# Tap sums of the late tokens' first chunks among the gates, layer norm statistics on VectorE, and a reordered convolution tail

## The reference, cut to what matters

```python
def conformer_conv_module(h, w_in, b_in, w_dw, b_dw, ln_g, ln_b, w_out, b_out):
    D = h.shape[-1]
    u = h @ w_in + b_in
    u = u[..., :D] * jax.nn.sigmoid(u[..., D:])
    u = lax.conv_general_dilated(            # 31 taps, each channel by itself, causal
        u, w_dw[:, None, :].astype(u.dtype), window_strides=(1,), padding=[(CONV_WIDTH - 1, 0)],
        dimension_numbers=('NWC', 'WIO', 'NWC'), feature_group_count=D) + b_dw
    u = jax.nn.silu(layer_norm(u, ln_g, ln_b))
    return u @ w_out + b_out
...
x = x + g1[:, None, :] * y                   # y is the module's output
h = modulate(rms_norm(x, norm2_g[layer]), sh2, sc2)
x = x + g2[:, None, :] * moe_ffn(h, ...)
```

## Time and profile before

| | before |
|---|---|
| median of 3 runs | 2340.85 us (2340.23 to 2343.32) |
| the profiled execution | 2344.01 us, span 2342.2 us |
| mean granted TensorE clock | 0.941 |
| busy: PE / DVE / ACT / POOL | 2095.6 / 1156.7 / 676.9 / 348.2 us |
| chain that ended last | PE 82%, DVE 8%, DMA 5%, ACT 2%, issue 2% |
| first gate product of DVE to the last router logits | 1356.5 to 1782.4 us of the span |

### The profile page before, as it was taken

How to read it: one execution, slowest core, us unless ns; L and a number is a source line. 1 busy time by engine, 2 the same in 40 slices (tenths; PEclk the granted TensorE clock), 3 DMA queues, 4 the chain that set the end, 5 groups by cost and what they waited for, 6 DMA issues and landing times.

```text
span 2342.2 us, 51476 instructions
## 1 busy us (share of the span) xinstructions
PE 2095.6 (89%) x19986; PEld 1150.2 (49%) x19987; DVE 1156.7 (49%) x2301; ACT 676.9 (29%) x1654; POOL 348.2 (15%) x609
## 2 busy tenths in 40 slices
PE   6999999999999579999999489997983899999991
PEld 2444444455666345555555367653442455555550
DVE  2355500578898532222322689997735222232225
ACT  3111100567777322222222310006252222222222
POOL 0000010000000122222222330000001222222223
PEclk9999999799999789999999699998986899999996
DMA  9266510103300746658776401232034777734746
GB/s 395 77 244 241 198 55 0 37 19 144 145 10 10 301 147 256 219 203 319 259 287 254 164 0 72 96 101 65 1 126 170 295 292 290 286 120 149 258 149 224
DMA packets 117719, 391.04 MB, mean 167 GB/s; under 512 B 22849, under 2 KB 43969, under 8 KB 112257
## 3 DMA queue, kind: packets, MB, share of 16 engines
q1 hardware_dynamic: 67970, 302.95, 34.1%
q0 software_dynamic: 21632, 67.76, 8.2%
q10 hardware_dynamic: 28032, 19.17, 2.7%
HBM read 337.56 MB, written 47.49 MB: 164 GB/s over the span
## 4 chain that ended last, share of the span: by engine, by line
PE 82%; DVE 8%; DMA 5%; ACT 2%; issue 2%; SPq 1%; POOL 0%; ACTq 0%; DVEq 0%; POOLq 0%
PE ps L1527 21%; PE ps L1541 11%; PE ps L1400 10%; PE ps L1600 7%; PE ps L1671 5%; PE ps L1418 5%; PE ps L1474 4%; PE ps L1432 3%; PE ps L1445 3%; PE ps L1457 3%; DVE kv L1267 3%; PE ps L1519 2%; DMA ring<-in_w_gate_up 2%; PE ps L1534 1%; PE ps L1347 1%
## 5 line engine op out<-in xcount | busy, mean ns | idle before, releaser
L1179 DVE TENSOR_TENSOR hT<-hT,ps 128x128 f32<-128x128 f32 x146 | 42.0, 288 | 546.1 <-ACT hT L732 546.1
L1527 PE MATMUL ps<-ring,hT 128*32 128x256 f32 x4544 | 267.3, 388 | 18.8 <-issue 9.1
L1527 PE MATMUL ps<-kv,hT 128*32 128x256 f32 x4800 | 276.2, 382 | 6.4 <-issue 3.1
L1267 DVE SCALAR_TENSOR_TENSOR kv<-kv,cols 128x640 f32<-128x640 f32 (+1 forms) x330 | 273.7, 829 | 11.2
L732 ACT ACTIVATE hT<-ps 128x128 f32<-128x128 f32 x146 | 40.4, 277 | 708.3 <-PE ps L1527 708.3
L1600 PE MATMUL ps<-hT,ring 128*128 128x320 f32 (+1 forms) x768 | 226.3, 456 | 8.1 <-ACT hT L617 8.1
L1400 PE MATMUL ps<-hT,ring 128*128 128x512 f32 x512 | 226.9, 602 | 1.6 <-ACT hT L617 1.6
L1527 PEld LDWEIGHTS ps<-ring,hT 128*32 128x32 f32 x4544 | 153.8, 112 | 108.3 <-issue 26.5
L1527 PEld LDWEIGHTS ps<-kv,hT 128*32 128x32 f32 x4800 | 155.7, 110 | 101.1 <-issue 10.3
L1016 DVE TENSOR_TENSOR_SCAN pbuf<-hT 128x128 f32<-128x128 f32 (+7 forms) x128 | 173.2, 1353 | 47.8 <-ACT hT L668 47.4
L725 ACT ACTIVATE hT<-ps,modc 128x32 f32<-128x32 f32 x592 | 175.2, 377 | 68.0 <-PE ps L1519 68.0
(11 more groups left out here) (255 smaller groups left out, 2432.9 us busy)
## 6 DMA issues: line engine op xcount, KB each, us to landing
ring<-in_w_gate_up SPq DMA_DIRECT2D x128, 512.0 KB
kv<-in_w_gate_up SPq DMA_DIRECT2D x128, 512.0 KB
kv<-in_w_ada SPq DMA_DIRECT2D x20, 2048.0 KB, 8.2
ring<-in_w_down SPq DMA_DIRECT2D x64, 512.0 KB
kv<-in_w_down SPq DMA_DIRECT2D x64, 512.0 KB
expert_rows<-hT ACTq DMA_DIRECT2D x584, 32.0 KB
ring<-in_w_in SPq DMA_DIRECT2D x8, 2048.0 KB, 8.3
expert_rows<-ring POOLq DMA_DIRECT2D x2, 7680.0 KB, 23.7
```

What stands on the lines that cost most here:

```text
L1267: ins = V.scalar_tensor_tensor(new, old, w_dw_c[:, c, k:k + 1], new, ALU.mult, ALU.add)
L1527: ins = mm(bank(0)[UNIT * q:UNIT * (q + 1), 0:2 * P], xT[:, c, :], wset[s][q // 2][:, 512 * c + 256 * (q % 2):512 * c + 256 * (q % 2) + 25 ...
```

## The change

The pairs that PE sums are now (0, 3) and (1, 0) to (1, 3), before (0, 7) and (1, 4) to (1, 7). Their `sum_taps` stand after gates 5, 10, 11 and 12; only the fifth follows the gates. DVE keeps eleven pairs, seven early and four late. `GATED_AT` and the order of turning are new. The mean and variance of the early tiles are made by DVE with the instructions of the late ones, inside its eighth pair. POOL no longer adds the bias; DVE makes `b_gated` and adds it to the eight tiles behind its last pair. `b_gated` is loaded to another place, after the last values. SP's shifted copies stand earlier in its queue. The late layer norm's scale and shift are made for three tiles at once, where they were made for one and then two, and the late tiles are turned back earlier among the outputs.

```diff
-SUMMED = [(0, 7), (1, 4), (1, 5), (1, 6), (1, 7)]
-VECTOR = [(0, c) for c in range(7)] + [(1, c) for c in range(4)]
...
-GATED_AT = {(0, 19): 1, (1, 6): 2, (1, 25): 3, (2, 13): 4, (3, 1): 5, (3, 19): 6, (4, 8): 7, (4, 19): 8, (4, 30): 9,
-            (5, 10): 10, (6, 1): 11, (6, 13): 12, (6, 23): 13, (7, 6): 14, (7, 30): 15}
-SCALED_AT = (8, 18)
-TURNED_AFTER = {2: 0, 4: 1, 6: 2, 7: 3, 10: 4, 11: 5, 13: 6, 14: 7}
-SUMMED_AFTER = {10: 0, 14: 1}
+SUMMED = [(0, 3), (1, 0), (1, 1), (1, 2), (1, 3)]
+VECTOR = [(0, c) for c in (0, 1, 2, 4, 5, 6, 7)] + [(1, c) for c in range(4, DC)]
...
+GATED_AT = {(0, 19): 1, (1, 6): 2, (1, 25): 3, (2, 12): 4, (2, 30): 5, (3, 27): 6, (4, 15): 7, (4, 26): 8, (5, 6): 9,
+            (5, 17): 10, (6, 3): 11, (6, 19): 12, (7, 8): 13, (7, 22): 14, (7, 26): 15}
+MEASURED_AT, SCALED_AT = (7, 24), (7, 28)
+TURNED_AFTER = {2: 0, 4: 1, 6: 2, 7: 3, 8: 4, 10: 5, 12: 6, 14: 7}
+SUMMED_AFTER = {5: 0, 10: 1, 11: 2, 12: 3}
...
             for j in range(10):
+                if j == 5:
+                    load_shifted(0)
                 if j == 7:
-                    load_shifted(0)
-                if j == 9:
                     for n in (1, 2, 3):
                         load_shifted(n)
+                if j == 8:
+                    load_shifted(4)
...
-            pool.wait_ge(h_made, 3 * TT)
-            pool.wait_ge(x_biased, 1)
-            for t in range(TT):
-                ins = nc.gpsimd.tensor_tensor(xtile(t), xtile(t), b_gated, ALU.add)
-            ins.then_inc(x_biased, 1)
...
             pool.wait_ge(values_done, 2 * DC)
-            make_taps(3)
-            pool.wait_ge(taps_summed, 3)
-            make_taps(4)
+            pool.dma_start(b_gated, b_out.partition_broadcast(P)).then_inc(bc_loaded, 16)
...
-            for t in range(FIRST):
-                after(nc.scalar.activation(junk, xt[0][:, t, :].rearrange("p (a b) -> p a b", a=2), ACT.Identity,
-                                           accum_out=ln_sum[:, t:t + 1]))
...
+                    if (d, k) == MEASURED_AT:
+                        for g in range(FIRST):
+                            statistics(g)
...
+            def add_bias(t):
+                step(V.tensor_tensor(xtile(t), xtile(t), b_gated, ALU.add))
...
+            step(V.tensor_tensor(b_gated, b_gated, bcC[:, :], ALU.mult))
+            for g in range(FIRST, TT):
+                statistics(g)
+            add_bias(0)
+            add_bias(1)
+            scales(FIRST, TILES[1])
```

More of the change, by code:

```diff
@@ L581, in _ @@
             pool.wait_ge(diag_made, 1)
+            pool.wait_ge(h_made, 3 * TT)
             make_taps(0)
-            for n in (1, 2):
+            for n in range(1, len(SUMMED)):
                 pool.wait_ge(taps_summed, n)
@@ L844, in _ @@
-            for t in range(FIRST):
-                after(nc.scalar.activation(junk, xt[0][:, t, :].rearrange("p (a b) -> p a b", a=2), ACT.Identity,
-                                           accum_out=ln_sum[:, t:t + 1]))
-            keep_taps(2)
-            keep_chunk(8)
-            after(nc.scalar.activation(ln_mean[:, 0:FIRST], ln_sum[:, 0:FIRST], ACT.Copy, scale=-D ** -1.5))
-            for t in range(FIRST):
-                after(nc.scalar.activation(junk, xt[0][:, t, :].rearrange("p (a b) -> p a b", a=2), ACT.Square,
-                                           scale=D ** -0.5, bias=ln_mean[:, t:t + 1], accum_out=ln_var[:, t:t + 1]))
@@ L857, in _ @@
-            for g in range(FIRST):
-                normalise(g)
+            act.wait_ge(ln_scaled, FIRST)
+            normalise(0)
+            normalise(1)
             activate(0)
+            normalise(2)
             activate(1)
             keep_taps(4)
-            keep_chunk(10)
-            activate(2)
-            keep_out(0)
-            keep_chunk(11)
-            activate(3)
-            keep_out(1)
-            keep_chunk(12)
+            normalise(3)
+            normalise(4)
+            keep_out(0)
@@ L1247, in gated, with statistics, scales @@
                                        ALU.mult).then_inc(u_done, 1)
+            def statistics(g):
+                h = g // FIRST
+                row = xt[h][:, g - FIRST * h, :]
+                dve.wait_ge(conv_kept, DC * (h + 1))
+                for j in range(2):
+                    ins = V.bn_stats(bn_part[:, j, :], row[:, 512 * j:512 * j + 512])
+                step(ins)
+                V.bn_aggr(bn_all[:, g, :], bn_part[:, :, :]).then_inc(bn_made, 1)
+                dve.wait_ge(bn_made, g + 1)
+            def scales(g, n):
+                dve.wait_ge(ln_root, g + n)
+                step(V.reciprocal(ln_rstd[:, g:g + n], ln_var[:, g:g + n]))
+                V.scalar_tensor_tensor(ln_shift[:, g:g + n], bn_all[:, g:g + n, 0], -1.0,
+                                       ln_rstd[:, g:g + n], ALU.mult, ALU.mult).then_inc(ln_scaled, n)
             gated(0)
@@ L1309, in _ @@
-            scales(FIRST + 1, 2)
-            add_output(2)
-            norm_scale(3, 1)
-            add_output(3)
+            for t in (2, 3):
+                add_bias(t)
+                add_output(t)
+            for t in range(4, TT - 1):
+                add_bias(t)
+            V.tensor_tensor(xtile(TT - 1), xtile(TT - 1), b_gated, ALU.add).then_inc(x_biased, 1)
+            add_output(4)
+            for t in range(4):
+                norm_scale(3, t)
+            add_output(5)
             norm_keep(3, 0)
-            add_output(4)
@@ L1731, in _ @@
             turn(3, 3)
+            turn(3, 4)
             project_out(7, 1)
-            turn(3, 4)
+            turn(3, 5)
             logits(3, 0)
-            for t in range(5, TT):
-                turn(3, t)
+            turn(3, 6)
+            turn(3, 7)
             logits(3, 1)
```

232 lines of the change are left out of this document (92 added, 140 removed).

## The result

| | before | after |
|---|---|---|
| median us (4 runs each) | 2342.09 | 2308.59 |
| lowest and highest us | 2340.23, 2343.73 | 2306.02, 2311.82 |
| ratio, 95% interval | | 0.986 (0.9848 to 0.9872) |
| profiled execution: time, span, clock | 2344.01, 2342.2, 0.941 | 2308.09, 2306.3, 0.949 |

The change takes 33.5 us off, by the medians; the forecast was 2311.

What follows compares the result with a forecast made beforehand. PE and DVE were both fully loaded in the gates, with bad hand-overs between them. Savings of 15.3 + 1.3 + 0.9 + 7.5 + 5.8 = 30.8 us from the 2340.85 median gave 2310.1, plus 1: 2311 us; range 2304 to 2324.

Steps and rivals of the forecast that it cites:

- First, the bias: Module start and DVE's first pair: with the bias off POOL, 1.8 us earlier start and 9.1 us less DVE stall.
- The net of 9.1 less 1.5: DVE's first pair: 9.1 us of stall goes, but POOL's first tap-set multiply, hidden in it, costs 1.5 again.
- The 1.8 of the start: Before PE's first gate: DVE's combination no longer slowed by POOL's `b_gated` multiply, so everything starts 1.8 us earlier.
- Second, VectorE's queue as the path to the scale: First gate product to early tiles' scale: DVE's queue is the longest path; scale 15.3 us earlier, at 1596.7.
- the 21 narrow taps fewer: DVE ahead of the early scale: scale at tap 28 of the eighth pair, not 18 of the ninth, -13.7 us.
- My "nothing" for ScalarE's statistics: Removing ACT's five sums and five squares costs nothing in time, since they lay beside DVE's taps.
- Third, SP: SP's queue among the gates: shifted copies and last weights arrive in time, by 1.6 us; cost 0, bounds 0 and 1.9.
- Fourth to sixth: From scale to last logits: early halves, late norm and tail with fewer waits; last logits at 1747.9, -30.8 us.
- Late hand-overs: Rival in the gates: missed values or copies cost 1 to 3 us each, up to 8: 2319; chance 0.14.
- a tail that keeps its length: Rival: the tail's waits come back elsewhere, 13 of the 30.8 us are lost: 2324; chance 0.11.
- SP's copies: Rival, slower: copies over 0.59 us delay gate 12's values; gain gone from 1.5 a copy, 2350 at 1.7; chance 0.03.
- The clock stays up: Rival: the gap before the first late half is too short to lower the clock, 3.1 us sooner: 2308; chance 0.08.

Runs made afterwards that it cites:

- experiment 5: The kernel before, with the bias product and eight bias additions moved from GpSimd to VectorE's tail and nothing else: 2327.73 us, ratio 0.995 to before.
- experiment 8: The kernel after, with the early tiles' statistics nine multiplications earlier on VectorE and the scale behind them: 2302.81 us, ratio 0.9841 to before.
- Experiment 3: The kernel after, with TensorE's sums 1 to 3 behind the last gate chunk instead of among the gates: 2322.98 us, ratio 0.9917 to before.
- experiment 2: The kernel after, with the statistics of the five early tiles on ScalarE again: 2315.25 us, ratio 0.9893 to before.
- experiment 1: The kernel after, with the bias product and the eight bias additions back on GpSimd: 2320.76 us, ratio 0.9909 to before.
- the kernel with all four moves: The kernel after, with earlier statistics, fifth sum ahead of the turns back, activation of tile 5 before an eviction, tile 6 in other banks: 2295.20 us.
- experiment 6: The kernel after, with TensorE's fifth sum ahead of the first two turns back instead of behind them: 2310.64 us, ratio 0.9872 to before.

## Why the prediction was right, and where it was off

In us from the MEMSET (the prediction's moments less 1354.4, its start):

| moment | before | predicted | after |
|---|---|---|---|
| scale of the early tiles ready | 255.7 | 242.3 | 241.7 |
| first turn back | 257.1 | 243.8 | 243.0 |
| early halves end | 343.1 | 328.2 | 326.4 |
| first late half starts | 349.7 | 333.9 | 332.3 |
| last half ends | 407.2 | 384.0 | 380.6 |
| last logits start | 422.6 | 393.5 | 390.2 |

- **First, the bias.** The mechanism is right. The net of 9.1 less 1.5 was 7.6; the first 19 taps gained 26.6 - 18.1 = 8.4, and undone it cost 8.6 to the first turn back. I had priced a pair's first tap at 0.92, where it takes 0.61, and the tap set's multiply beside it at 1.5, where the first tap took 1.57 - 0.61 = 1.0 longer. The 1.8 of the start reached TensorE's first gate whole; that the MEMSET came only 0.9 sooner, against the same reciprocal, is the slower clock in that gate, which I had left out. That the module begins at 1354.38, as the sum had it, is luck: 0.8 us of it were there before the first change.
- **Second, VectorE's queue as the path to the scale.** Right within 0.6 us, and experiment 5 shows it for the kernel before too. Its largest term, the 21 narrow taps fewer, was not undone by itself; experiment 8 shows the same mechanism one step further. My "nothing" for ScalarE's statistics was right, but not because VectorE's place is free of cost: where I put them back they cost 6.4.
- **Third, SP.** No wait for copies or weights. The four late sets of 16 copies held SP for 10.26, 11.36, 10.02 and 10.02 us. The slow copy that I feared was there: in the second set two copies took 2.56 us together instead of 1.22, and a pair of that set took 1.84 to 2.83 in the profiles of all the kernels that kept this order. It was covered, since the third set had to wait 1.7 us for the first late sum. The weights landed 9.5 us after their issue at 1534.10, about 1 us before they were wanted, where I had 1.6. So the hand-over held by little. Experiment 3 shows what the order guards against.
- **Fourth to sixth.** The hand-overs are as told: 9.56 us of TensorE's idle time against "about 11", 4.12 against 3.9, none in the tail. What was mis-sized is the clock. I gave the first half 8.8 us and the late half 10.1, as before; they took 7.13 and 8.73. That is 1.7 + 1.4 of the 3.3 us by which the last row of the table lies under the forecast; 0.8 more was won ahead of the first turn back, and the other terms give 0.6 back (0.3 of it a slip: the parts from 1598.2 on add up to 1682.9, not 1682.6). For the first half the sum contradicts itself: it takes away the wait of 1.9 ahead of it and keeps the slow half that stood behind that wait. The row in the kernel before:

```profile
1625.27 8.83 PE L1671 MATMUL ps<-ring,hT 128*128 128x512 f32 x16 [1.94 <-ACT kv L801]
```

The clock was 1.00 from 1616.7 until that wait, and 0.50 from 1627.3 to 1629.3. The late half of 10.1 was one reading: the same place, behind waits of 3.9 to 4.1 us, took 8.57 to 9.20 in seven other executions.
- **The rivals.** Late hand-overs, a tail that keeps its length and SP's copies did not happen. "The clock stays up" happened for the first half, for which I had not named it, and not for the late half, which was slow for a shorter time. The total of 2308.59 meets that rival's 2308 by these two shares, not by its own mechanism.
- **The rest** of the difference between the two profiled spans (35.9) is 0.9 at the start, 0.8 ahead of that, where nothing is changed, and 1.7 behind the last logits (563.5 to 561.8). The part behind the logits took 559.9 to 562.9 in the other kernels' profiles, so the 1.7 is not credited to the change.

The parts don't add up: undone one at a time they cost 9.95 + 6.4 + 13.4 + 13.8 = 43.6 us, and together they brought 32.4. Experiments 2 and 3 also hold ScalarE up at places of their own, and the single shares are not shown to be what each part brought. Experiment 5 gained 12.1 where experiment 1 lost 9.95, and the clock accounts for the difference: 8.4 + 3.7 there, 8.6 + 1.3 here. To the first turn back the move of the bias is worth the same in both kernels.

## What to carry to other kernels

Walk the engine that never stands still, and price every step by its place on it: the same five statistics cost 7.8 us on the busy engine and still beat the old placement on ScalarE by 6.4, and moving them nine taps up gained 6.1 more. Before moving work off an engine because it comes late there, see whether a buffer alone makes it late (experiment 2). The sum placed in the wait did most where it filled it to the end: the clock stayed up, and the turns back took 1.97 us (the kernel with all four moves). Where it left a gap of 4.26 us behind it, the clock fell and took back 1.4 us of the 3.8 (experiment 6). Measure a stretch between two fixed instructions where the rest of the program drifts by more than the effect.

## What the runs showed of the hardware

- GpSimd additions of 128x1024 (eight in 19.9 us, the last 10.6 beside taps) slow VectorE's instructions beside them from 0.92 us a tap to up to 2.85, by 8.4 us in all, the tap set's multiply of 2.49 us behind them included; moved to VectorE they take 1.22 each. One such GpSimd multiply beside VectorE's combination put TensorE's first gate off by 1.8 to 2.0 us.
- A wait that leaves TensorE idle for 4.1 us was followed by a granted clock down to 0.59 for some us. Behind one of 1.8 us the half took 7.10 to 7.11 us in three places where the clock had been up for long, and 8.52 where the turns back ahead of it had run at 0.50. Behind one of 1.94, with the clock up for only some 6.5 us ahead of it, it took 8.83. How soon the clock returns behind the same wait differs between executions (8.57 to 10.09 us for one half, 10.71 to 11.95 for the first gate).
- 24 idle matmuls of 128x128 (5.5 us, where the wait was 4.1) kept it up, at 1.7 us of gain for the half behind them. That they pay where they fit into the wait is not shown.
